# Dense products that read x alternately from its two halves, evictions that put the tokens back in order

## The chip, the core and the metric

The kernel runs on one core of a Trainium2 chip. The metric is the device time of the whole program in microseconds: the median of several runs. A profiled execution of the same program supplies the trace that is read here.

## What is computed

One inference step of a decoder layer, for 256 prompt tokens and 8 sample tokens together (264 tokens). Cut to what matters here, with every tensor in float32:

```
x += 0.5 * (silu(h @ w_gate) * (h @ w_up)) @ w_down      # h = rms_norm(x); w_gate, w_up 2048 x 5632
P  = rms_norm(x) @ w_in                                  # 2048 x 6400
mix = concat(attention(P), rwkv7(P), conv(P))
x += mix @ w_out                                         # 2048 x 2048
x += 0.5 * (silu(h @ w_gate2) * (h @ w_up2)) @ w_down2
```

The outputs are x for both groups of tokens and the new attention, RWKV and convolution states.

## The kernel before

The activations lie transposed in SBUF, features on partitions and the 264 tokens along the row: `xr` is x, `pj` the projection P, `hH` and `hL` the hidden layer, `mixH` and `mixL` the mixed heads. Each dense operand is held as two fp32r tensors, a high part and the rest (`xH` and `xL`, `wH` and `wL`), and a product is the sum of three matmuls: high with high, low with high, high with low (L378, L379, L380; or L339 for the part of the output projection that is prepared ahead during the RWKV stage).

Weights stream from HBM in chunks of up to 4 x 128 rows by 256 columns through a ring of four slots. For each chunk SyncE issues the load into `raw`, ScalarE makes `wH` (L310), VectorE makes `wL` (`tail`, L365), and TensorE works through it in `products`: for each of up to four row blocks q and two column halves, three matmuls, each with its own 128x128 weight load and the 264 tokens as moving operand. A chunk of 4 x 128 rows is 24 matmuls. The semaphore `tail_made` lets TensorE start a chunk; `chunk_used` frees the slot for ScalarE and the loads.

A gate/up pair is four chunks into PSUM banks 0 and 1 (gate) and four into banks 2 and 3 (up). An output pair of the down projection is twelve chunks, one of the input or output projection four. Banks alternate, so that a pair's results are read out while the next pair is being computed. The read-outs are on VectorE: `gate_scale` (L458, writes `gt`), `hidden` (L466, writes `ut`), `project` (L712, writes `pj`), `x_add` (L430, adds to `xr`) and `y_add` (L696, writes `yf` for the last stage). Each reads two banks of 264 columns. VectorE has one queue: tails and read-outs stand in it in the order of the program. Squares, heads and tails of x (`squares`, `x_heads`, `x_tails`) follow each `x_add`, and `turn_y` transposes each `yf` (L827, L829).

The dense matmuls already go through the tokens from the last column to the first: operand and output both have a step of -1. Other matmuls (the sums for the norm, attention, RWKV) go forwards; among them is L1183, a plain f32 product of a 128x128 block with 264 columns.

Of the kernel before, what the change touches and what calls it, by code (L numbers as in the profile page):

```python
# [20 lines left out]
ALU = mybir.AluOpType  # L21
# [8 lines left out]
N = T + NB  # L30
# [22 lines left out]
OUT_K0 = (0, 12, 4, 8)  # L53
# [57 lines left out]
def build(nc, t, o):  # L111
# [4 lines left out]
    def at(name, shape, dt, off):  # L116

        return nc.alloc_sbuf_tensor_at(name, shape, dt, offset=base + off)
# [5 lines left out]
    xr = at("xr", [P, KT, N], F32, 49152)  # L124
# [6 lines left out]
    gt = at("gt", [P, 2, N], F32, E0)  # L131
    st = at("st", [P, 2, N], F32, E0 + 2112)
    ut = at("ut", [P, 2, N], F32, E0 + 4224)
# [4 lines left out]
    rs = at("rs", [P, N], F32, K0)  # L138
# [16 lines left out]
    yf = at("yf", [P, 2, 2, N], F32, M0 + 92928 + 6144)  # L155
# [6 lines left out]
    pj = at("pj", [P, MT, N], F32, PB)  # L162
# [81 lines left out]
    def inner_slots(*ks):  # L244
# [18 lines left out]
    ahead = {k: (at(f"wH{k}", [P, CK, CW], F32R, hi), at(f"wL{k}", [P, CK, CW], F32R, lo))  # L263
             for k, hi, lo in ((0, F0, F0 + 8192), (1, F0 + 4096, PB + G), (2, L0 + 4 * HB, L0 + 4 * HB + 4096),
                               (3, L0 + 4 * HB + 8192, L0 + 4 * HB + 12288),
                               (6, PB + 2 * G, PB + 2 * G + 4096), (7, PB + 2 * G + 8192, PB + 2 * G + 12288))}
# [7 lines left out]
    ps = ctx.enter_context(nc.psum_tensor("ps", [P, 8, 512], F32))  # L274
    sems = {}

    def S(name):
        if name not in sems:
            sems[name] = ctx.enter_context(nc.semaphore(name))
        return sems[name]  # L280
# [13 lines left out]
    def number(first, per, i, k):  # L294

        return i * per + (first + k)
# [28 lines left out]
    def pe_ahead(pe, k, qs=range(CK)):  # L325

        pe.wait_ge(S("tail_made"), OUT + k + 1)
        for q in qs:
            for half in range(2):
                ahead_product(k, q, half, 0, mixH, k % 4 == 0 and q == 0)  # L330
                ahead_product(k, q, half, 0, mixL)
                last = ahead_product(k, q, half, 1, mixH, stop=k == 7 and q == CK - 1)
        if CK - 1 in qs:
            last.then_inc(S("chunk_used"), 1)

    def ahead_product(k, q, half, part, mix, start=False, stop=False):

        cols = slice(half * P, half * P + P)
        return nc.tensor.matmul(ps[:, 4 + k // 4 * 2 + half, 0:N][:, ::-1], ahead[k][part][:, q, cols],  # L339
                                mix[:, OUT_K0[k % 4] + q, :][:, ::-1], start=start, stop=stop)  # L340

    def pe_ahead_rwkv(pe):

# [18 lines left out]
    def tail(dve, nk, first, per, i, k):  # L362
# [3 lines left out]
                                wH[:, k % RING, 0:nk, :].bitcast(F32), ALU.subtract  # L366
                                ).then_inc(S("tail_made"), 1)

    def products(pe, vH, vL, k0, nk, bank, start, stop, first, per, i, k):

        pe.wait_ge(S("tail_made"), number(first, per, i, k) + 1)
        for q in range(nk):
            for half in range(2):
                cols = slice(half * P, half * P + P)
                out = ps[:, bank + half, 0:N][:, ::-1]
                high, low = vH[:, k0 + q, :][:, ::-1], vL[:, k0 + q, :][:, ::-1]
                a, b = start and q == 0, stop and q == nk - 1
                nc.tensor.matmul(out, wH[:, k % RING, q, cols], high, start=a, stop=False)  # L378
                nc.tensor.matmul(out, wH[:, k % RING, q, cols], low, start=False, stop=False)  # L379
                last = nc.tensor.matmul(out, wL[:, k % RING, q, cols], high, start=False, stop=b)  # L380
        last.then_inc(S("chunk_used"), 1)

    def two(ap):

        return ap[:].unsqueeze(1).broadcast_to([P, 2, N])
# [6 lines left out]
    def early(q):  # L392

        return isinstance(q, int) and q < 2
# [32 lines left out]
    def x_add(dve, w, q, bank, factor, used):  # L427

        dve.wait_ge(S("chunk_used"), used)
        nc.vector.scalar_tensor_tensor(xr[:, bass.ds(q * 2, 2), :], ps[:, bank:bank + 2, 0:N], factor,  # L430
                                       xr[:, bass.ds(q * 2, 2), :], ALU.mult, ALU.add
                                       ).then_inc(S("x_ready"), 1)

    def norm_sum(pe, w):

# [19 lines left out]

    def gate_scale(dve, u, first, p):
        dve.wait_ge(S("chunk_used"), first + 4 + p * GU_PER)
        nc.vector.tensor_tensor(gt[:], ps[:, 0:2, 0:N], two(rs), ALU.mult).then_inc(S("gate_scaled"), 1)  # L458

    def gate_silu(act, u, p):  # L460
        act.wait_ge(S("gate_scaled"), FT // 2 * u + 1 + p)
# [1 line left out]

    def hidden(dve, u, first, p):
        dve.wait_ge(S("chunk_used"), first + GU_PER + p * GU_PER)
        nc.vector.tensor_tensor(ut[:], ps[:, 2:4, 0:N], two(rs), ALU.mult).then_inc(S("up_scaled"), 1)  # L466
        dve.wait_ge(S("up_scaled"), FT // 2 * u + 1 + p)
        dve.wait_ge(S("silu_made"), FT // 2 * u + 1 + p)
        nc.vector.tensor_tensor(hf[:], st[:], ut[:], ALU.mult).then_inc(S("hidden_made"), 1)
# [171 lines left out]
    def dve_ffn(dve, u, gu, dn):  # L641
        def gate_up(i, first_pair):
            for k in range(RING if first_pair and u == 0 else 0, 4):
                tail(dve, CK, gu, GU_PER, i, k)
            if not first_pair:
                hidden(dve, u, gu, i - 1)
            elif u == 1:
                x_add(dve, 2, KT // 2 - 1, 6, 1.0, GU2)
            tail(dve, CK, gu, GU_PER, i, 4)
            if not first_pair:  # L650
                hidden_tail(dve, u, i - 1)
            elif u == 1:
                x_tails(dve, 2, KT // 2 - 1)
            for k in range(5, GU_PER):
                tail(dve, CK, gu, GU_PER, i, k)
            if first_pair:
                norm_reciprocal(dve, 2 * u)
            gate_scale(dve, u, gu, i)
# [32 lines left out]
    def y_add(dve, q, slot, used):  # L691

        dve.wait_ge(S("chunk_used"), used)
        if not early(q):
            dve.wait_ge(S("y_turned"), q - 1)
        nc.vector.scalar_tensor_tensor(yf[:, slot, :, :], ps[:, 4 + 2 * slot:6 + 2 * slot, 0:N], 0.5,  # L696
                                       xr[:, bass.ds(q * 2, 2), :], ALU.mult, ALU.add
                                       ).then_inc(S("x_ready"), 1)

    def column_pair(q):  # L700

# [2 lines left out]
    def seat(q):  # L704

        return 2 * column_pair(q) + (-6 if 16 <= q < 19 else 6 if q >= 22 else 0)

    def project(dve, q, bank):

        dve.wait_ge(S("chunk_used"), IN + IN_PER + q * IN_PER)  # L710
        c = seat(q)
        nc.vector.tensor_tensor(pj[:, c:c + 2, :], ps[:, bank:bank + 2, 0:N], two(rs), ALU.mult  # L712
                                ).then_inc(S("projected"), 1)

    def dve_in(dve):
        for k in range(4):
            tail(dve, CK, IN, IN_PER, 0, k)
        x_add(dve, 1, KT // 2 - 1, 6, 0.5, IN)
        x_tails(dve, 1, KT // 2 - 1)
        for k in range(4):  # L720
# [55 lines left out]
    def pe_ffn(pe, u, gu, dn):  # L776
        w = 2 * u

        def gate_up(i, first_pair):
            for k in range(GU_PER):  # L780
                if first_pair and k < 4:
                    pe.wait_ge(S("x_tail"), 16 * w + 4 * (k + 1))
                if k == 0 and not first_pair:
                    pe.wait_ge(S("gate_scaled"), FT // 2 * u + i)
                if k == 4 and not first_pair:
                    pe.wait_ge(S("up_scaled"), FT // 2 * u + i)
                products(pe, xH, xL, CK * (k % 4), CK, 0 if k < 4 else 2, k % 4 == 0, k % 4 == 3,
                         gu, GU_PER, i, k)
                if first_pair and u == 0 and k == 0:
                    pe_turn_x(pe, 6)  # L790
                    pe_turn_x(pe, 7)
                if first_pair and k == (5 if u == 0 else 3):
                    norm_sum(pe, w)

        def down(i, jj, first_pair):
            q = i * 2 + jj
            if not (isinstance(i, int) and i == 0):
                pe.wait_ge(S("x_ready"), 8 * (w + 1) - 1 + q)
            for k in range(DN_PER):
                if first_pair:  # L800
                    pe.wait_ge(S("hidden_tail"), FT // 2 * u + (DN_K0[k] + DN_KT[k] + 1) // 2)
                products(pe, hH, hL, DN_K0[k], DN_KT[k], 4 + 2 * jj, k == 0, k == DN_PER - 1,
                         dn + DN_PER * jj, 2 * DN_PER, i, k)
                if u == 1 and not first_pair and k == 5:
                    turn_y(pe, q - 1, 1 - jj)
# [26 lines left out]
    def pe_in(pe):  # L832
        for k in range(4):
            pe.wait_ge(S("x_tail"), 16 + 4 * (k + 1))
            products(pe, xH, xL, CK * k, CK, 0, k == 0, k == 3, IN, IN_PER, 0, k)
# [1651 lines left out]
```

## Time and profile before

| | |
|---|---|
| median of 3 runs | 2109.93 us (2109.79 to 2113.65) |
| span of the profiled execution | 2106.7 us |
| TensorE busy | 2074.8 us, 98% |
| VectorE busy | 1183.1 us, 56% |
| ScalarE busy | 880.0 us, 42% |
| mean load rate from HBM and to it | 177 GB/s |

The page gives no other time of the profiled execution than its span; the median stands 3.2 us above it. Matmuls are pipelined: one of 284 ns starts every 120 ns or so, so that a busy share of TensorE says little, and the distance from one start to the next says more. The span falls into gate and up of the first FFN (to about 541 us), its down projection (to 802), the input projection with attention beside it (to about 1065), the RWKV stage (to 1256), the output projection (to 1339), and the second FFN (gate and up to 1838, down to 2101).

### The profile page before, as it was taken

How to read it: one execution, taken by the hardware profiler on the slowest of the kernel's cores; microseconds unless marked ns; L12 is line 12 of the kernel's file. 1: busy time of each engine (PE TensorE's matmuls, PEld its weight loads, DVE VectorE, ACT ScalarE, POOL GpSimd, SP SyncE). 2: the span in 40 equal slices, each digit the busy share in tenths (PEclk: the TensorE clock that was granted, in tenths of full speed). 3: DMA queues.
4: the chain of work that ended last, by engine and by line, in shares of the span. 5: the costliest groups of instructions: out<-in, count | busy, mean ns of one | idle time of the engine just before them, and what ended most of it. 6: DMA issues, size and time to landing. Idle time of an engine off the chain costs nothing.

```text
span 2106.7 us, 44887 instructions
## 1 busy us (share of the span) xinstructions
PE 2074.8 (98%) x18520; PEld 2038.6 (97%) x18520; DVE 1183.1 (56%) x1203; ACT 880.0 (42%) x1004; POOL 196.9 (9%) x160
## 2 busy tenths in 40 slices
PE   8999999999999999999998999999999999999999
PEld 7999999999999999999986899999999999999999
DVE  6555555555444545568996575555555555544443
ACT  5444444444434434434345444444444444433333
POOL 4000000000000000015401871000000000000000
PEclk9999999999999999999998999999999999999999
DMA  5655555665555556668873055555556555556553
GB/s 184 197 182 180 179 180 179 185 182 180 176 179 177 187 172 199 175 201 221 238 237 88 4 165 190 180 180 180 181 179 186 179 179 180 183 166 196 185 176 125
DMA packets 361375, 373.43 MB, mean 177 GB/s; under 512 B 13321, under 2 KB 353837, under 8 KB 361190
## 3 DMA queue, kind: packets, MB, share of 16 engines
q1 hardware_dynamic: 352288, 350.53, 53.5%
q0 software_dynamic: 5424, 15.39, 3.1%
q10 hardware_dynamic: 3582, 6.33, 0.9%
q8 instruction: 63, 1.03, 0.2%
q14 instruction: 18, 0.15, 0.0%
HBM read 366.89 MB, written 5.32 MB: 177 GB/s over the span
## 4 chain that ended last, share of the span: by engine, by line
PE 89%; DVE 5%; DMA 3%; ACT 1%; POOL 1%; issue 1%; ACTq 0%; SPq 0%; POOLq 0%; DVEq 0%
PE ps L378 28%; PE ps L380 28%; PE ps L379 28%; DMA raw<-in_w_in_dram 2%; DVE wL L365 2%; DVE wL L323 1%; POOL acc L888 1%; PE ps L1266 1%; PE ps L1955 0%; DMA vb<-in_cache_swa_v_dram 0%; ACT wH L310 0%; PE ps L1958 0%; DMA xin<-in_x_prompt_dram 0%; PE ps L1966 0%; PE ps L339 0%
## 5 line engine op out<-in xcount | busy, mean ns | idle before, releaser
L365 DVE TENSOR_TENSOR wL<-raw,wH 128x1024 fp32r<-128x1024 f32 (+1 forms) x668 | 824.2, 1240 | 829.3 <-ACT wH L310 828.5
L310 ACT ACTIVATE wH<-raw 128x1024 fp32r<-128x1024 f32 (+1 forms) x668 | 691.2, 1037 | 966.4 <-PE ps L380 888.0
L378 PE MATMUL ps<-xH,wH 128*128 128x264 f32 x3616 | 1030.2, 285 | 6.2 <-DVE wL L365 5.8
L380 PE MATMUL ps<-xH,wL 128*128 128x264 f32 x3616 | 1027.3, 284 | 0.0
L379 PE MATMUL ps<-xL,wH 128*128 128x264 f32 x3616 | 1027.2, 284 | 0.0
L378 PEld LDWEIGHTS ps<-xH,wH 128*128 128x128 f32 x3616 | 681.3, 188 | 11.3 <-issue 9.7
L380 PEld LDWEIGHTS ps<-xH,wL 128*128 128x128 f32 x3616 | 681.1, 188 | 0.0
L379 PEld LDWEIGHTS ps<-xL,wH 128*128 128x128 f32 x3616 | 680.5, 188 | 0.2
L378 PE MATMUL ps<-hH,wH 128*128 128x264 f32 x1408 | 402.4, 286 | 0.0
L380 PE MATMUL ps<-hH,wL 128*128 128x264 f32 x1408 | 401.4, 285 | 0.0
L379 PE MATMUL ps<-hL,wH 128*128 128x264 f32 x1408 | 401.3, 285 | 0.0
L378 PEld LDWEIGHTS ps<-hH,wH 128*128 128x128 f32 x1408 | 265.0, 188 | 0.2
L379 PEld LDWEIGHTS ps<-hL,wH 128*128 128x128 f32 x1408 | 265.1, 188 | 0.0
L380 PEld LDWEIGHTS ps<-hH,wL 128*128 128x128 f32 x1408 | 264.6, 188 | 0.0
L462 ACT ACTIVATE st<-gt 128x528 f32<-128x528 f32 x44 | 28.5, 647 | 83.6 <-DVE gt L458 83.6
L888 POOL TENSOR_TENSOR acc<-acc,sq 128x528 f32<-128x528 f32 x21 | 34.9, 1663 | 278.0 <-ACT sq L406 277.0
L378 PE MATMUL ps<-mixH,wH 128*128 128x264 f32 x192 | 54.5, 284 | 0.0
L379 PE MATMUL ps<-mixL,wH 128*128 128x264 f32 x192 | 54.5, 284 | 0.0
L380 PE MATMUL ps<-mixH,wL 128*128 128x264 f32 x192 | 54.5, 284 | 0.0
L890 POOL COPY acc<-sq 128x528 f32<-128x528 f32 x3 | 2.7, 894 | 552.5 <-ACT sq L406 549.7
L421 DVE SCALAR_TENSOR_TENSOR xL<-xr,vcol,xH 128x264 fp32r<-128x264 f32 (+1 forms) x48 | 29.9, 664 | 15.6 <-ACT xH L413 15.4
L380 PEld LDWEIGHTS ps<-mixH,wL 128*128 128x128 f32 x192 | 36.1, 188 | 0.0
(377 smaller groups left out, 1140.3 us busy)
## 6 DMA issues: line engine op xcount, KB each, us to landing
raw<-in_ffn_w_gate_dram SPq DMA_DIRECT2D x176, 512.0 KB, 3.5
raw<-in_ffn_w_up_dram SPq DMA_DIRECT2D x176, 512.0 KB, 3.5
raw<-in_ffn_w_down_dram SPq DMA_DIRECT2D x128, 512.0 KB, 3.3
raw<-in_w_in_dram SPq DMA_DIRECT2D x100, 512.0 KB, 4.9
raw<-in_ffn_w_down_dram SPq DMA_DIRECT2D x64, 384.0 KB, 2.8
raw<-in_w_out_dram SPq DMA_DIRECT2D x32, 512.0 KB, 4.4
kb<-in_cache_swa_k_dram POOLq DMA_DIRECT2D x24, 256.0 KB, 6.6
vb<-in_cache_swa_v_dram ACTq DMA_DIRECT2D x24, 256.0 KB, 6.4
```

Of the source, the lines that this page charges most:

```text
L310: nc.scalar.activation(wH[:, k % RING, 0:nk, :], raw[:, k % RING, 0:nk, :], ACT.Copy).then_inc(S("head_made"), 1)
L323: nc.vector.tensor_tensor(low[:], raw[:, k % RING], high[:].bitcast(F32), ALU.subtract).then_inc(S("tail_made"), 1)
L365: nc.vector.tensor_tensor(wL[:, k % RING, 0:nk, :], raw[:, k % RING, 0:nk, :], wH[:, k % RING, 0:nk, :].bitcast(F32), ALU.subtract).then_i ...
L378: nc.tensor.matmul(out, wH[:, k % RING, q, cols], high, start=a, stop=False)
L379: nc.tensor.matmul(out, wH[:, k % RING, q, cols], low, start=False, stop=False)
L380: last = nc.tensor.matmul(out, wL[:, k % RING, q, cols], high, start=False, stop=b)
L421: nc.vector.scalar_tensor_tensor(xL[:, bass.ds(q * 2 + e, 1), :], xr[:, bass.ds(q * 2 + e, 1), :], vcol[:, 0, bass.ds(q * 2 + (16 * w + e) ...
L462: nc.scalar.activation(st[:], gt[:], ACT.Silu).then_inc(S("silu_made"), 1)
L888: nc.gpsimd.tensor_tensor(acc[:], acc[:], sq[:, slot, :, :], ALU.add).then_inc(S("squares_added"), 1)
L890: nc.gpsimd.tensor_copy(acc[:], sq[:, 0, :, :]).then_inc(S("squares_added"), 1)
L1266: last = nc.tensor.matmul(ps[rows, 4, :], pS[:, g, b, :], vb[:, b % 3, g, :], start=g == 0, stop=g == 2)
```

## The change

In `products` and `ahead_product`, the moving operand is read from the last column to the first with the two halves of the tokens taking turns: 263, 131, 262, 130, down to 132, 0. `two_ways` makes that access pattern. PSUM is written as before, column 263 first and column 0 last, each neighbour to neighbour. So bank columns 2c and 2c+1 hold tokens c and 132+c. The five read-outs read every second column (`by_token`) and write two runs of 132 tokens (`by_way`), which puts the tokens in their order. `x_add` and `y_add` become two VectorE instructions each, one for each bank. Nothing else is changed: loads, splits, semaphores and the order of the queues are the same.

```
     def ahead_product(k, q, half, part, mix, start=False, stop=False):
-        return nc.tensor.matmul(ps[:, 4 + k // 4 * 2 + half, 0:N][:, ::-1], ahead[k][part][:, q, cols],
-                                mix[:, OUT_K0[k % 4] + q, :][:, ::-1], start=start, stop=stop)
+        return nc.tensor.matmul(ps[:, 4 + k // 4 * 2 + half, 0:N][:, ::-1].rearrange("p (c way) -> p c way", way=2), ahead[k][part][:, q, cols],
+                                two_ways(mix[:, OUT_K0[k % 4] + q, :]), start=start, stop=stop)
...
+    def two_ways(ap):
+        return ap[:, ::-1].rearrange("p (way c) -> p c way", way=2)
+
+    def by_token(bank):
+        return ps[:, bank:bank + 2, 0:N].rearrange("p e (c way) -> p e way c", way=2)
+
+    def by_way(ap):
+        return ap.rearrange("p e (way c) -> p e way c", way=2)
...
-                out = ps[:, bank + half, 0:N][:, ::-1]
-                high, low = vH[:, k0 + q, :][:, ::-1], vL[:, k0 + q, :][:, ::-1]
+                out = ps[:, bank + half, 0:N][:, ::-1].rearrange("p (c way) -> p c way", way=2)
+                high, low = two_ways(vH[:, k0 + q, :]), two_ways(vL[:, k0 + q, :])
...
     def x_add(dve, w, q, bank, factor, used):
-        nc.vector.scalar_tensor_tensor(xr[:, bass.ds(q * 2, 2), :], ps[:, bank:bank + 2, 0:N], factor,
-                                       xr[:, bass.ds(q * 2, 2), :], ALU.mult, ALU.add
-                                       ).then_inc(S("x_ready"), 1)
+        for e in range(2):
+            tile = by_way(xr[:, bass.ds(q * 2 + e, 1), :])[:, 0]
+            last = nc.vector.scalar_tensor_tensor(tile, by_token(bank)[:, e], factor, tile, ALU.mult, ALU.add)
+        last.then_inc(S("x_ready"), 1)
...
-        nc.vector.tensor_tensor(gt[:], ps[:, 0:2, 0:N], two(rs), ALU.mult).then_inc(S("gate_scaled"), 1)
+        nc.vector.tensor_tensor(by_way(gt[:]), by_token(0), by_way(two(rs)), ALU.mult).then_inc(S("gate_scaled"), 1)
...
-        nc.vector.tensor_tensor(ut[:], ps[:, 2:4, 0:N], two(rs), ALU.mult).then_inc(S("up_scaled"), 1)
+        nc.vector.tensor_tensor(by_way(ut[:]), by_token(2), by_way(two(rs)), ALU.mult).then_inc(S("up_scaled"), 1)
...
-        nc.vector.scalar_tensor_tensor(yf[:, slot, :, :], ps[:, 4 + 2 * slot:6 + 2 * slot, 0:N], 0.5,
-                                       xr[:, bass.ds(q * 2, 2), :], ALU.mult, ALU.add
-                                       ).then_inc(S("x_ready"), 1)
+        for e in range(2):
+            last = nc.vector.scalar_tensor_tensor(by_way(yf[:, slot])[:, e], by_token(4 + 2 * slot)[:, e], 0.5,
+                                                  by_way(xr[:, bass.ds(q * 2 + e, 1), :])[:, 0], ALU.mult, ALU.add)
+        last.then_inc(S("x_ready"), 1)
...
-        nc.vector.tensor_tensor(pj[:, c:c + 2, :], ps[:, bank:bank + 2, 0:N], two(rs), ALU.mult
+        nc.vector.tensor_tensor(by_way(pj[:, c:c + 2, :]), by_token(bank), by_way(two(rs)), ALU.mult
                                 ).then_inc(S("projected"), 1)
```

## Rows read from the trace of the kernel before

**Rows 1.** The page: span, and busy time of each engine
```profile
span 2106.7 us, 44887 instructions
...
PE 2074.8 (98%) x18520; PEld 2038.6 (97%) x18520; DVE 1183.1 (56%) x1203; ACT 880.0 (42%) x1004; POOL 196.9 (9%) x160
```

**Rows 2.** Busy time by stretches: length, then each engine, granted clock, DMA share, GB/s
```profile
48.00:540.00 492.00, 492.00 (x4071) 492.00 (x4072) 264.77 (x258) 204.09 (x214) 0.00 (x0) 1.00 0.60 183
545.00:800.00 255.00, 255.00 (x2092) 255.00 (x2091) 124.03 (x119) 104.75 (x120) 13.63 (x9) 1.00 0.56 180
930.00:1065.00 135.00, 128.88 (x1069) 125.80 (x1068) 116.23 (x105) 52.67 (x65) 56.58 (x57) 1.00 0.84 240
```

**Rows 3.** Waits: who waited for whom, us in total, times, longest
```profile
ACT wH L310 <- PE ps L380: 888.0, 542, 3.7
DVE wL L365 <- ACT wH L310: 828.5, 575, 6.1
...
PE ps L378 <- DVE wL L365: 5.8, 5, 2.5
```

**Rows 4.** Groups of instructions by form, whole span
```profile
L378 PE MATMUL ps<-xH,wH 128*128 128x264 f32 x3616 | 1030.2, 285 | 6.2 <-DVE wL L365 5.8
L378 PE MATMUL ps<-hH,wH 128*128 128x264 f32 x1408 | 402.4, 286 | 0.0
L378 PE MATMUL ps<-mixH,wH 128*128 128x264 f32 x192 | 54.5, 284 | 0.0
L712 DVE TENSOR_TENSOR pj<-ps,rs 128x528 f32<-128x528 f32 x25 | 17.5, 700 | 11.4 <-PE ps L380 11.3
L430 DVE SCALAR_TENSOR_TENSOR xr<-ps,xr 128x528 f32 x12 | 8.4, 700 | 0.0
L339 PE MATMUL ps<-mixH,wH 128*128 128x264 f32 x64 | 16.2, 292 | 2.1 <-DVE wL L323 2.0
```

**Rows 5.** Busy time by stretches, as rows 2, in short windows
```profile
15.30:19.00 3.70, 3.70 (x17) 3.70 (x18) 3.17 (x6) 2.63 (x5) 0.00 (x0) 0.50 0.53 164
100.00:200.00 100.00, 100.00 (x830) 100.00 (x829) 52.42 (x51) 41.34 (x43) 0.00 (x0) 1.00 0.59 179
600.00:700.00 100.00, 100.00 (x821) 100.00 (x821) 49.18 (x48) 41.08 (x47) 5.38 (x3) 1.00 0.56 182
1700.00:1800.00 100.00, 100.00 (x830) 100.00 (x829) 54.32 (x54) 41.77 (x44) 0.00 (x0) 1.00 0.59 180
```

**Rows 6.** Chain that ended last, 886 to 889 us: start, duration, what
```profile
887.02 1.78 PE ps L1183 x8
```

**Rows 7.** Timeline from 304.4 us, TensorE and VectorE
```profile
304.60 1.22 DVE L365 TENSOR_TENSOR wL<-raw,wH 128x1024 fp32r<-128x1024 f32 x1 [1.72 <-ACT wH L310]
...
305.18 0.29 PE L379 MATMUL ps<-xL,wH 128*128 128x264 f32 x1
305.31 0.29 PE L380 MATMUL ps<-xH,wL 128*128 128x264 f32 x1
305.44 0.28 PE L378 MATMUL ps<-xH,wH 128*128 128x264 f32 x1
```

**Rows 8.** Single lines of VectorE: duration min/median/max in ns, starts, form
```profile
L2377 DVE COPY yo<-ps x1: 245/245/245, 1220.7 to 1220.7; 128x48 f32<-128x48 f32 x1
L1360 DVE COPY vcol<-ps x1: 221/221/221, 878.2 to 878.2; 128x68 f32<-128x68 f32 x1
L1381 DVE COPY qkr<-ps x1: 277/277/277, 930.1 to 930.1; 96x128 f32<-96x128 f32 x1
L1808 DVE SCALAR_TENSOR_TENSOR kk<-ps,vcol,pj x6: 482/482/485, 1133.7 to 1135.7; 128x264 f32<-128x264 f32 x6
```

**Rows 9.** Timeline from 2101 us
```profile
2101.39 0.71 DVE L696 SCALAR_TENSOR_TENSOR yf<-ps,xr 128x528 f32<-128x528 f32 x1 [6.95 <-PE ps L380]
```

**Rows 10.** Groups of TensorE, 930 to 1065 us
```profile
L378 PE MATMUL ps<-xH,wH 128*128 128x264 f32 x323 | 92.6, 287 | 3.6 <-DVE wL L365 3.5
```

## Prediction

> **What bounds the kernel now.** I read the page first: span and engine shares [rows 1]. TensorE is busy 98% of 2106.7 us; VectorE 56%, ScalarE 42%. Busy time of pipelined matmuls doesn't tell whether the engine is at its limit, so I went to the table by stages [rows 2]. In gate/up (the second FFN repeats the first) TensorE is busy every microsecond, 4071 matmuls in 492 us, 120.9 ns from one to the next; in the down stretches 2092 in 255 us, 121.9 ns, all at the full granted clock (1.00). The waits of TensorE say the same from the other side: over the whole run L378 waits 5.8 us for VectorE's low halves [rows 3]. While it streams, nothing holds it up but its own pace. The exception is 930 to 1065 us (end of the input projection beside attention): the DMA share is 0.84, TensorE is idle for 6 us [rows 2], and 3.5 of the 5.8 us of waiting fall there [rows 10].
>
> The reader is to see one number: the **pitch** of a dense matmul, start to start. There are 3 x (3616 + 1408 + 192 + 64) = 15,840 of them (each count is that of one of three equal rows, shown for L378 and L339) [rows 4]. One hundred undisturbed microseconds hold 830 (120.5 ns) in gate/up and 821 (121.8 ns) in down [rows 5]. So the dense products take about 1,915 of 2,107 us, and 1 ns of pitch is worth 15.8 us. Everything else in this change is small beside that.
>
> **What the pitch is made of.** 264 columns at 2.4 GHz, one a period, are 110 ns. Three rows stand around the measured 120.5.
> - At the half clock (granted 0.50, so 1.2 GHz) 17 of the same instructions fall into 3.7 us [rows 5], some 218 ns each. 264/1.2 is 220: no excess at all.
> - The plain f32 product of the same shape (L1183: 128x128 stationary, 264 columns, own weight load, read forwards) takes 1.78 us for eight [rows 6], 222.5 ns, or twice 111. It needs two periods for a column and has 1 ns of excess per 264 periods.
> - The dense product at full clock wants a new 4-byte column each period and pays 120.5: 9.3 ns above 111.2.
>
> So the excess shows only where operands are wanted at the highest rate. It also moves with SBUF traffic of others: against the 120.5 of the average, starts stand 0.13 us apart (305.18, 305.31, 305.44) half a microsecond after VectorE's tail (raw and wH in, wL out) has started at 304.60 [rows 7]. The excess therefore looks like fetching, not counting. The order of the moving read is what the change alters.
>
> **The change, part by part.**
>
> 1. Moving read. For each of the 15,840 matmuls, column 263 comes first, then 131, then 262, 130 and so on: neighbours in the stream stand 528 bytes apart instead of 4. Number of columns, bytes, weight loads, start/stop flags and waits are unchanged. The trace has no dense matmul with such a read, so I bound its price. From below: the whole excess goes, -9.3 ns each, pitch 111.2. From above: each column takes two periods, as the columns of L1183 do and as those at the half clock do: 220 ns [rows 5, 6]. VectorE gives a hint for the upper end: its copy of 48 values to places 1056 bytes apart takes 245 ns (L2377), while contiguous copies out of PSUM take 221 ns for 68 values (L1360) and 277 for 128 (L1381) [rows 8]. A contiguous value costs 1.06 ns there: (700 - 277)/(528 - 128), from L430 [rows 4] and L1381. At that slope 48 contiguous values would take 200 ns, so L2377 pays 45 ns more: 0.9 ns per far-stepped value, nearly one more of its own steps. This is a write of another engine; no row has a far-stepped read on TensorE.
>
> The Trainium skill (Advanced Engine Details and Errata, section Memory Cachelines) speaks against this change: SBUF is read in lines of 16 bytes, and at least two hits on a line are needed to absorb its latency, with a penalty when each access is to another line. By it every column here would be a new line, and the pitch would be the upper end. The row of VectorE agrees with its direction, no row here tests it for TensorE.
>
> For the other side: now one walk through x advances by a value in every period. The alternate order makes two walks, one per half, and each advances only every second period. If the engine can keep a place in both, whatever it fetches per walk has twice the time, and the 9.3 ns shrink. I take half of them, 4.6 ns, as the likeliest gain, because no row lies between no effect and all: pitch 115.9 in gate/up.
>
> 2. PSUM write. Still column 263 down to 0, neighbours adjacent, same bank: the access pattern is merely written as pairs. 0.
>
> 3. Evictions in token order. gt, ut (44 each) and pj (25) keep their count; they read PSUM at a step of two values. Now 700 ns each (pj, and the others in the same form) [rows 4]; between +0 and, at a further period for each value as above, +0.55 us. In gate/up that is at most 2 x 0.55 in the 23.2 us of a pair (192 x 120.9 ns), of which VectorE is busy 54% (264.8 of 492) [rows 2]; it would be 59%. What stands behind them in VectorE's queue is the next chunk's tail, and tails wait 828.5 us in total for ScalarE, who waits 888.0 for TensorE [rows 3]: each has over a microsecond of slack in 2.9. Cost 0; if that cover were gone, at most 113 x 0.55 = 62 us.
>
> 4. x_add (16) and y_add (8) become two instructions of 264 values. Now 700 ns; the nearest 264-value instruction on PSUM, L1808, is 482 ns, six of them start 2.0 us from first to last, 0.4 apart [rows 8]. Two are about 0.88 us, +0.2 each, 5 us of VectorE in all. 23 lie beside products (the bank they free is wanted a whole column pair later). The last y_add doesn't: TensorE ends, yf takes 0.71, the turn waits for it [rows 9]. +0.2, and up to +0.5 for the PSUM step. I take +0.5 in sum with the two stage changes.
>
> 5. DMA, semaphores, POOL: untouched. If TensorE speeds up by 4%, the 180 GB/s of gate/up become 187; 240 have been moved in 930 to 1065 [rows 2]. In that stretch, though, its 970 dense products (3 x 323) [rows 10] share the queues with 240 GB/s of loads, and TensorE already waits for tails; I count no gain.
>
> **Sum.** 14,870 x -4.6 ns = -68.4; +0.5; span 2106.7 becomes 2038.8. The median 2109.9 of the runs lies 3.2 above the profiled span (the page has no other time of that execution), so 2042.
>
> **Rivals.**
> - A, faster (the forecast). For it: the 9.3 ns exist, vanish at the half clock, and grow when VectorE uses SBUF. Against: no row shows that a second place can be held. Own range 1980 (all but 1 ns of excess gone: 14,870 x -8.5 = -126) to 2100. Chance 0.45.
> - B, half-rate read, on the other side. Each column is a fetch of its own and TensorE gets one every second period: pitch 220 for all that now have 121.2 on average. 15,840 x 98.8 = +1565, 3675; if a third of the present 9.3 ns stays on top of it, 49 us more, 3725. It decides as soon as what the engine holds of x serves only neighbours in the stream. For it: the write of L2377. Against: it is another engine's. Everything else would be hidden beneath it: the load rate falls to about 100 GB/s. Chance 0.35. It is also what the line rule of the Trainium skill named above would do here.
> - C, the order doesn't matter, the excess belongs to something else (for one, to swapping weights): +0.5 us, 2110.4. For it: three stretches far apart, with 16 different rows of x, weights from four slots and loads landing all the time, hold 830, 821 and 830 products [rows 5]; collisions of addresses would scatter more. Chance 0.12.
> - D, more collisions without half rate: every product takes what those beside VectorE's tails take now, 125 instead of 121: +4 x 15,840 = +63, 2173. Chance 0.08.
>
> **How the numbers follow.** 0.2% of the time is 4.2 us, about what a measurement of this kernel can tell from no change. A and its whole range give faster; B and D slower; C same: 0.45, 0.12, 0.43. Leaving out B would leave out more than 2 in 10, so the range reaches from A's low end to B: 1980 to 3730. It is wide because the outcomes are two islands; A's own range is 1980 to 2100.
>
> **What would show it.** The decisive view is the count of matmuls in 100 us of gate/up: 830 now; 863 for A, about 455 for B, 830 for C, 800 for D, with the clock still granted in full. In down: 821 becomes 853 or about 455. The duration of a single matmul (284 ns) would shrink by the same 4.6 ns in A and grow by 100 in B. VectorE's gt, ut and pj at 700 show part 3 right; at 1.25 us, its upper bound. x_add in two pieces near 0.45 shows part 4. In B the waits of ScalarE for TensorE would more than double from 888 us and the idle 6 us of 930 to 1065 vanish. The prediction is wrong at its root if the pitch goes up: then half of the excess wasn't there to take, and the read pays for every far step.

## Result and the profile after

The changed kernel takes 1987.95 us (median of 4 runs, 1986.01 to 1989.46) against 2109.96 before: a ratio of 0.9417, 95% interval 0.9404 to 0.943, or 122 us less. That is the direction of rival A and lies in its own range of 1980 to 2100, near the lower end: the gain is 1.8 times the 68 us that were forecast. The profiled execution has a span of 1984.2 us.

The page of the changed kernel, busy time by engine:

```profile
span 1984.2 us, 44915 instructions
PE 1942.3 (98%) x18520; PEld 1904.6 (96%) x18520; DVE 1183.9 (60%) x1227; ACT 881.5 (44%) x1004; POOL 196.7 (10%) x160
```

The number of matmuls is the same (18,520), VectorE has 24 instructions more and the same busy time (1183.1 before [rows 1]). TensorE is 98% busy in both kernels, so the busy share doesn't show the gain at all. The count of matmuls in a stretch does. Busy time by stretches of the changed kernel (length, then TensorE, weight loads, VectorE, ScalarE, POOL, granted clock, DMA share, GB/s):

```profile
48.00:540.00 492.00, 492.00 (x4375) 492.00 (x4375) 282.46 (x276) 219.97 (x231) 1.15 (x1) 1.00 0.64 196
545.00:730.00 185.00, 185.00 (x1647) 185.00 (x1646) 97.47 (x99) 81.51 (x93) 10.64 (x6) 1.00 0.60 194
```

and in windows of 100 us, which answer to [rows 5]:

```profile
100.00:200.00 100.00, 100.00 (x892) 100.00 (x891) 56.17 (x54) 44.40 (x47) 0.00 (x0) 1.00 0.63 194
600.00:700.00 100.00, 100.00 (x891) 100.00 (x890) 52.14 (x53) 43.11 (x49) 5.36 (x3) 1.00 0.59 193
1600.00:1700.00 100.00, 100.00 (x892) 100.00 (x891) 57.60 (x57) 45.26 (x47) 0.00 (x0) 1.00 0.65 194
```

In 492 us there are 4375 matmuls instead of 4071 [rows 2], so the pitch fell from 120.9 to 112.5 ns (a window counts those that reach over its edges too, so over 100 us the quotient comes out 0.3 to 0.4 ns too small: the starts themselves were 120.8 and 122.0 ns apart on average where the quotients of [rows 5] give 120.5 and 121.8). Gate/up and down now have the same pitch; before, down was 1 ns slower. And it no longer varies. Timeline of the changed kernel, TensorE beside a tail of VectorE:

```profile
305.17 0.28 PE L391 MATMUL ps<-xL,wH 128*128 128x264 f32 x1
305.28 0.28 PE L392 MATMUL ps<-xH,wL 128*128 128x264 f32 x1
305.40 0.28 PE L390 MATMUL ps<-xH,wH 128*128 128x264 f32 x1
305.51 0.28 PE L391 MATMUL ps<-xL,wH 128*128 128x264 f32 x1
305.62 0.28 PE L392 MATMUL ps<-xH,wL 128*128 128x264 f32 x1
305.67 1.22 DVE L365 TENSOR_TENSOR wL<-raw,wH 128x1024 fp32r<-128x1024 f32 x1 [1.48 <-ACT wH L310]
305.73 0.28 PE L390 MATMUL ps<-xH,wH 128*128 128x264 f32 x1
305.85 0.28 PE L391 MATMUL ps<-xL,wH 128*128 128x264 f32 x1
305.96 0.28 PE L392 MATMUL ps<-xH,wL 128*128 128x264 f32 x1
```

Starts are 0.11 or 0.12 us apart before and during the tail; the 0.13 of [rows 7] are gone. In the starts of the trace from 100 to 200 us and from 600 to 700 us, every gap is 112 or 113 ns; before, they were 118 to 129. 264 columns at 2.4 GHz are 110 ns, so 2.5 ns are left above one column a period. (The Trainium skill, TensorE: Matmul & The Clock Gate, section Back-to-back issue gap, gives N/2.4 + 2.5 ns as the gap of an isolated matmul at the full clock, and says that a stream in which each matmul has its weight load departs from it. By the isolated rule 264 columns give 112.5 ns; this stream, with a weight load for each matmul, shows just that.)

**The variation before was not VectorE's doing.** The prediction took the 0.13 us beside a tail for traffic of VectorE. Starts stand as far apart in the down projection with VectorE idle. Timeline of the kernel before, TensorE and VectorE:

```profile
755.50 1.22 DVE L365 TENSOR_TENSOR wL<-raw,wH 128x1024 fp32r<-128x1024 f32 x1 [1.45 <-ACT wH L310]
...
756.77 0.29 PE L378 MATMUL ps<-hH,wH 128*128 128x264 f32 x1
756.90 0.28 PE L379 MATMUL ps<-hL,wH 128*128 128x264 f32 x1
...
757.51 0.28 PE L378 MATMUL ps<-hH,wH 128*128 128x264 f32 x1
...
757.69 1.23 DVE L365 TENSOR_TENSOR wL<-raw,wH 128x1024 fp32r<-128x1024 f32 x1 [0.96 <-ACT wH L310]
```

From 756.77 to 757.51 there are six matmuls, 123 ns each, and VectorE does nothing from 756.72 to 757.69. In gate/up the gaps repeat every 96 matmuls, which is four chunks, once through the 16 rows of x and the four slots of the ring: their standard deviation is 1.7 ns over all and 0.1 ns among those at the same place of this cycle (matmuls 400 to 4,200 of the trace). In down they repeat every 264, once through the 44 rows of the hidden layer: 2.3 ns over all, 0.3 at the same place. In gate/up two thirds of all gaps are exactly 120 ns. At two places half a cycle apart the gap is 122.7 and 122.6 ns on average, though VectorE works at the first in all of 41 rounds and at the second in none. Beside tails the mean is 121.4 ns and with VectorE idle 120.3, because the tails come at the same places of the cycle each time, and those are among the slow ones. So in gate/up the excess over two walks is 7.5 ns (120 less 112.5) at most places, and up to 7 ns more at some, which goes with the operands of that place. In down only one gap in eight is 120 ns, and more are above it. Whether the row of x, the place of the weights or something else that repeats with them makes the difference wasn't looked into.

**Where the 122 us come from.** The first sum for the norm of each stage (L439 before, L452 after) marks the stages. It starts at 804.63 and 1339.15 us before:

```profile
804.63 0.61 PE L439 MATMUL ps<-acc,ones 128*128 128x264 f32 x2
...
1339.15 0.61 PE L439 MATMUL ps<-acc,ones 128*128 128x264 f32 x2
```

and at 749.88 and 1271.14 after:

```profile
749.88 0.39 PE L452 MATMUL ps<-acc,ones 128*128 128x264 f32 x1
...
1271.14 0.61 PE L452 MATMUL ps<-acc,ones 128*128 128x264 f32 x2
```

Up to the first mark 54.8 us are saved; between the marks (input projection, RWKV stage, output projection) 534.5 have become 521.3, 13.3 less; behind the second, up to the end of the span, 767.5 have become 713.1, 54.5 less. Together 122.5.

The middle gives less than its share. Groups of TensorE in the stretch up to 1065 us before and up to 1003 us after, which hold the same 1,952 dense products:

```profile
L378 PE MATMUL ps<-xH,wH 128*128 128x264 f32 x651 | 186.5, 287 | 3.6 <-DVE wL L365 3.5
```

```profile
L390 PE MATMUL ps<-xH,wH 128*128 128x264 f32 x651 | 183.3, 282 | 10.7 <-DVE wL L365 10.5
```

The first took 260 us (from 805), the second 252.5 (from 750.5): 7.5 us less, where 1,952 x 8.4 ns would be 16.4. Busy time by stretches shows what took the rest. Before and after:

```profile
805.00:1065.00 260.00, 253.88 (x2089) 250.18 (x2088) 191.16 (x166) 103.84 (x112) 59.35 (x62) 1.00 0.73 211
```

```profile
750.50:1003.00 252.50, 241.49 (x2086) 237.02 (x2086) 190.53 (x165) 102.63 (x111) 59.07 (x62) 0.99 0.75 217
...
867.00:1003.00 136.00, 124.99 (x1068) 121.10 (x1067) 115.98 (x104) 51.96 (x64) 56.31 (x57) 0.97 0.83 238
...
930.70:936.60 5.90, 5.86 (x27) 5.89 (x28) 5.90 (x3) 1.82 (x2) 5.10 (x4) 0.50 0.92 259
```

All of the loss is in the second part. By their starts, the 984 products up to 930 us before (867 after) gave 8.3 us, 8.4 ns each. The 968 products behind them, the stretch of 930 to 1065 us before [rows 2], took 136.1 us instead of 135.1: nothing gained, and 1 us lost. TensorE is idle for 11.0 instead of 6.1 us there: a faster consumer waits more for the tails (10.5 instead of 3.5 us), while its wait for attention's scores fell from 2.6 to 0.3 us. Waits in that part of the changed kernel:

```profile
ACT wH L310 <- DMA raw<-in_w_in_dram: 70.2, 26, 8.4
...
DVE wL L365 <- ACT wH L310: 19.5, 9, 7.1
...
PE ps L390 <- DVE wL L365: 10.5, 9, 2.9
```

ScalarE waits for the loads, VectorE for ScalarE, and TensorE for VectorE. The stretch moved 240 GB/s before and moves 238 now, so it looks bound by its loads and not by the pitch; no run tests that. VectorE also has attention's instructions ahead of some tails in its queue: one of 1.75 us stands right before the tail that starts at 929.38. Behind one of these waits the granted clock is 0.50 (1.2 GHz), and matmuls start 0.22 us apart; TensorE had stood idle for 2.9 us just before:

```profile
927.61 0.28 PE L392 MATMUL ps<-xH,wL 128*128 128x264 f32 x1
930.74 0.56 PE L390 MATMUL ps<-xH,wH 128*128 128x264 f32 x1 [2.85 <-DVE wL L365]
931.09 0.42 PE L391 MATMUL ps<-xL,wH 128*128 128x264 f32 x1
...
933.95 0.42 PE L392 MATMUL ps<-xH,wL 128*128 128x264 f32 x1
934.17 0.42 PE L390 MATMUL ps<-xH,wH 128*128 128x264 f32 x1
```

27 of them at 220 instead of 112.5 ns are 2.9 us. 4.9 and 2.9 account for 7.8 of the 8.9 us that are missing (16.4 less 7.5); the last microsecond isn't explained.

### The profile page after: what moved, and what is told of

Its sections match the earlier page's. It is cut to its first block, busy times and chain, and to the rows that moved or that the text cites. A ratio compares the mean times of both kernels' runs of the same rounds, so it can differ in the third digit from the quotient of the medians.

```text
span 1984.2 us, 44915 instructions
## 1 busy us (share of the span) xinstructions
PE 1942.3 (98%) x18520; PEld 1904.6 (96%) x18520; DVE 1183.9 (60%) x1227; ACT 881.5 (44%) x1004; POOL 196.7 (10%) x160
## 4 chain that ended last, share of the span: by engine, by line
PE 88%; DVE 6%; DMA 3%; ACT 1%; issue 1%; POOL 1%; ACTq 0%; SPq 0%; DVEq 0%; POOLq 0%
PE ps L390 27%; PE ps L392 27%; PE ps L391 27%; DVE wL L365 3%; DMA raw<-in_w_in_dram 2%; DVE wL L323 1%; POOL acc L902 1%; PE ps L1280 1%; PE ps L1969 0%; DMA vb<-in_cache_swa_v_dram 0%; PE ps L1972 0%; DMA xin<-in_x_prompt_dram 0%; ACTq L1340 0%; PE ps L1980 0%; ACT wH L310 0%
## 5 line engine op out<-in xcount | busy, mean ns | idle before, releaser
L390 PE MATMUL ps<-xH,wH 128*128 128x264 f32 x3616 | 1004.2, 278 | 14.7 <-DVE wL L365 14.5
L391 PE MATMUL ps<-xL,wH 128*128 128x264 f32 x3616 | 1000.0, 277 | 0.0
L392 PE MATMUL ps<-xH,wL 128*128 128x264 f32 x3616 | 999.9, 277 | 0.0
L390 PE MATMUL ps<-hH,wH 128*128 128x264 f32 x1408 | 389.2, 276 | 0.0
L391 PE MATMUL ps<-hL,wH 128*128 128x264 f32 x1408 | 388.6, 276 | 0.0
L392 PE MATMUL ps<-hH,wL 128*128 128x264 f32 x1408 | 388.6, 276 | 0.0
L390 PEld LDWEIGHTS ps<-mixH,wH 128*128 128x128 f32 x192 | 36.3, 189 | 0.0
```

## Experiments

Each edit changes only the access patterns of the dense matmuls, in `products` and `ahead_product`. `read` makes the moving operand from a row of x (264 values) and `write` the place in PSUM; before, both are `ap[:, ::-1]`. Where the two don't match and the read-outs don't put it right, the tokens come out in the order of the stream and are scaled by the norms of others; what is timed is the same work: as many matmuls of the same shape. e9 to e12 read some tokens twice and others not at all. All but e4 were run once, so their differences are read from the pitch: the verdict is the count of matmuls in gate/up, 100 to 200 us. The question behind them: what about the alternate order is it that counts?

### e1: one walk, forwards

```
-    return ap[:, ::-1]        # read and write
+    return ap
```

> Dense products read x and write PSUM from the first column to the last, one walk, everything else as before. Theory S (the stream's order): what the engine holds of x while it fetches is used up by neighbours in the stream; the direction of a single walk is of no account, pitch 120 to 122 ns, time within 20 us of before. Rival N (the negative step is itself a part of the gain): pitch above 122 ns, 123 to 130, 2140 to 2220 us.

2123.8 us (before beside it 2111.7).

```profile
100.00:200.00 100.00, 100.00 (x819) 100.00 (x818) 53.24 (x52) 40.96 (x44) 0.00 (x0) 1.00 0.58 178
600.00:700.00 100.00, 100.00 (x826) 100.00 (x825) 49.52 (x47) 41.08 (x48) 5.42 (x3) 1.00 0.56 183
```

819 in 100 us: the starts are 122.5 ns apart on average in gate/up (120.8 before), and 121.4 in down, where it is a little faster than before (122.0; 826 against 821). The direction of one walk is worth 12 us, a tenth of what the second walk is worth. That lies within theory S's 20 us and below theory N's 2140, but the direction isn't quite of no account; why backwards is better in one stage and worse in the other wasn't looked into.

### e2: the order of before, in two levels

```
+    return ap[:, ::-1].rearrange("p (c two) -> p c two", two=2)     # read and write
```

> The order of before (263, 262, 261, ...) written as a two-level access pattern of 132 pairs, for x and for PSUM, with the read-outs of before. It tells the form of the instruction from the order of the tokens. If the order is the cause: 830 matmuls in 100 us of gate and up, 120.5 ns, 2110 us. If the two-level pattern itself were the cause: 112.5 ns, 1988 us.

2110.9 us.

```profile
100.00:200.00 100.00, 100.00 (x830) 100.00 (x829) 53.59 (x52) 40.74 (x43) 0.00 (x0) 1.00 0.58 182
```

830, exactly as before. The form of the access pattern does nothing; the order does.

### e3: two walks, forwards

From the changed kernel, `two_ways` and `out` (`ahead_product` alike):

```
-    return ap[:, ::-1].rearrange("p (way c) -> p c way", way=2)
+    return ap.rearrange("p (way c) -> p c way", way=2)
...
-    out = ps[:, bank + half, 0:N][:, ::-1].rearrange("p (c way) -> p c way", way=2)
+    out = ps[:, bank + half, 0:N].rearrange("p (c way) -> p c way", way=2)
```

> The two halves still take turns, but both walks and PSUM run from the first column to the last (0, 132, 1, 133, ...), with the read-outs of the changed kernel. Theory S: 112.5 ns, 1988 us, as backwards. Rival N: the backward walk is needed for a part of it, 114 to 120 ns, 2010 to 2100 us.

1987.5 us.

```profile
100.00:200.00 100.00, 100.00 (x892) 100.00 (x891) 56.20 (x54) 44.41 (x47) 0.00 (x0) 1.00 0.64 194
```

With two walks the direction is of no account: 892 as in the changed kernel.

### e4: the read-outs alone

The changed kernel's read-outs with the products of before.

```
...
+    out = ps[:, bank + half, 0:N][:, ::-1]
+    high, low = vH[:, k0 + q, :][:, ::-1], vL[:, k0 + q, :][:, ::-1]
```

> x is read as before; only the read-outs are those of the changed kernel (every second column of PSUM, x_add and y_add in two pieces), so they leave the tokens permuted. It gives the price of the read-outs by themselves. The prediction has +0.5 us, ratio 1.000; if the step of two values cost VectorE a further period a value, gt would take 1.25 us and the time rise by 1 to 10 us.

2109.7 us; the ratio to before is 0.9994, 95% interval 0.9984 to 1.0004. Groups of VectorE in it:

```profile
L479 DVE TENSOR_TENSOR ut<-ps,rs 128x528 f32<-128x528 f32 x44 | 30.9, 701 | 0.0
L471 DVE TENSOR_TENSOR gt<-ps,rs 128x528 f32<-128x528 f32 x44 | 30.8, 701 | 0.1
...
L444 DVE SCALAR_TENSOR_TENSOR xr<-ps,xr 128x264 f32 (+1 forms) x32 | 12.2, 423 | 0.0
L710 DVE SCALAR_TENSOR_TENSOR yf<-ps,xr 128x264 f32<-128x264 f32 x16 | 6.1, 424 | 6.9 <-PE ps L392 6.9
```

Reading every second column of PSUM costs VectorE nothing that shows: 701 ns against 700 [rows 4]. The halves of x_add and y_add take 423 each. So the whole gain is the products'. That it is the read's, and not the pattern in PSUM's, e9 and e10 show below: they change the read alone and have all of it.

### e5 to e8: what must not be far, and from what

Four other orders of the read, everything else as before. The rival theories, in the names of the expectations: L, two lanes that take the values of the stream in turn, each holding the piece of 16 bytes that it used last; H, one holder of the last two pieces; B, collisions of neighbours in the same place.

```
e5  read: ap[:, ::-1].rearrange("p (way c two) -> p c way two", way=2, two=2)
e6  read: ap[:, ::-1].rearrange("p (c way) -> p way c", way=2)
e7  read: ap[:, ::-1].rearrange("p (c way) -> p way c", way=4)
e8  read: ap[:, ::-1].rearrange("p (way c) -> p c way", way=4)
```

> The two halves take turns by pairs of tokens (263, 262, 131, 130, 261, 260, ...); PSUM and the read-outs as before, so the tokens come out in the order of the stream, scaled by other tokens' norms. Theory L (two lanes: values 0, 2, 4, ... of the stream are fetched by one lane and 1, 3, 5, ... by another, and each holds the one 16-byte piece of x that it used last): each lane now jumps between the halves with every value, 264 fetches instead of 132 of before and 66 of after: well above 120.5 ns, up to 220, 2200 to 3700 us. Theory H (the engine holds the last two pieces, whichever value asks): 66 fetches as after, 112.5 ns, 1988 us. Theory B (neighbours of the stream that lie in the same place collide): between before and after, 116 ns, 2050 us.

2903.6 us, 581 in 100 us, 173 ns:

```profile
100.00:200.00 100.00, 100.00 (x581) 100.00 (x580) 37.22 (x37) 29.21 (x31) 0.00 (x0) 1.00 0.41 127
```

> One walk over every second token, then one over the others (263, 261, ..., 1, 262, ..., 0; 8 bytes between neighbours, two values of each 16-byte piece in a row); PSUM and read-outs as before, tokens left in the stream's order. Theory L: each lane takes one value of a piece, 264 fetches, as slow as e5. Theory H: 132 fetches, about the 120.5 ns of before. Theory B: other places, 112.5 to 116 ns.

3993.5 us, 417 in 100 us:

```profile
100.00:200.00 100.00, 100.00 (x417) 86.75 (x416) 26.24 (x26) 21.38 (x22) 0.00 (x0) 1.00 0.29 89
```

and its timeline, 0.24 us from start to start at the full clock (more than half of the gaps are exactly 240 ns, the mean is 241):

```profile
299.82 0.44 PE L387 MATMUL ps<-xL,wH 128*128 128x264 f32 x1
300.06 0.44 PE L388 MATMUL ps<-xH,wL 128*128 128x264 f32 x1
300.30 0.44 PE L386 MATMUL ps<-xH,wH 128*128 128x264 f32 x1
```

> One walk over every fourth token, four times (16 bytes between neighbours, each value in another 16-byte piece); PSUM and read-outs as before, tokens left in the stream's order. Theories L and H both: 264 fetches, well above 120.5 ns, up to 220 ns and 3700 us, and for L the same as e6. Theory B: 112.5 ns, since no two neighbours share a piece.

4038.6 us, 411 in 100 us, 244 ns:

```profile
100.00:200.00 100.00, 100.00 (x411) 85.94 (x410) 25.95 (x25) 20.32 (x21) 0.00 (x0) 1.00 0.29 90
```

> Four quarters of the tokens take turns (263, 197, 131, 65, 262, ...; 264 bytes between neighbours); PSUM and read-outs as before, tokens left in the stream's order. Theory L: each lane alternates between two quarters, 264 fetches, as slow as e5. Theory H: four walks are more than two held pieces, 264 fetches. Theory B: 112.5 ns as after, or less if room is left below it.

2442.2 us, 701 in 100 us, 143 ns:

```profile
100.00:200.00 100.00, 100.00 (x701) 100.00 (x700) 45.48 (x45) 34.41 (x36) 0.00 (x0) 1.00 0.50 153
```

e6 decides against H: two neighbours of its stream share a 16-byte piece, as those of before do, yet it takes twice as long. e7 and e6 decide against B: none of e7's neighbours share a place, and it is the slowest. In both each value of the stream is 16 bytes or more from the one two places before it, and both take 240 to 244 ns: nearly as slow as each other, as L has it, and slower still than the 220 that was given as its end. But L also wants e5 and e8 to be as slow, and they are not. So L holds in part: in a single walk the distance between value s and value s + 2 of the stream counts. Where value s + 2 lies in another walk the price is in between. Either something beyond the last piece is kept, or fetches overlap in part; the runs don't tell these apart.

### e9 to e12: does the distance between the walks count?

```
e9   read: offset + 259, steps [-1, 132], [-128, 2]
e10  read: offset + 135, steps [-1, 132], [-4, 2]
e11  read: offset + 77,  steps [-1, 66],  [-4, 4]
e12  read: offset + 139, steps [-2, 66],  [-8, 2], [-1, 2]
```

> Two walks of 132 as after, but 128 tokens (512 bytes) apart instead of 132 (528 bytes): 259, 131, 258, 130, ...; tokens 128 to 131 are read twice and 260 to 263 not at all; PSUM and read-outs as before. Theory L (each of two lanes takes every second value of the stream and does best on a walk of 4-byte steps): the distance is of no account, 112.5 ns, 1988 us. Rival P (the two places must lie in different parts of SBUF, which 528 bytes bring about and a round distance may not): above 112.5, up to the 240 of the single walk.

1987.1 us:

```profile
100.00:200.00 100.00, 100.00 (x891) 100.00 (x890) 56.18 (x54) 44.42 (x46) 0.00 (x0) 1.00 0.65 194
```

> Two walks as after, only 4 tokens (16 bytes) apart: 135, 131, 134, 130, ...; tokens 4 to 131 are read twice, those from 136 on not at all; PSUM and read-outs as before. Theory L: 112.5 ns, 1988 us, as 528 bytes. Rival P: the two walks are always in neighbouring pieces, as the single walks of e6 and e7 were, which took 240 ns: above 120.5.

1987.8 us:

```profile
100.00:200.00 100.00, 100.00 (x891) 100.00 (x890) 56.30 (x55) 44.37 (x46) 0.00 (x0) 1.00 0.63 194
```

> Four walks as in e8 (143 ns), but 4 tokens (16 bytes) apart instead of 66: 77, 73, 69, 65, 76, ...; tokens 0 to 77 are read again and again, the rest not; PSUM and read-outs as before. Each lane changes between two pieces 32 bytes apart. e8 was quicker than the 240 ns of e6 and e7, though each lane needs a new piece for each value there too. Theory F (fetches overlap where they go to places far apart): here they are near, about 240 ns, 4000 us. Theory M (a lane remembers a little more than its last piece, wherever it lies): 143 ns as e8, 2440 us.

2428.0 us:

```profile
100.00:200.00 100.00, 100.00 (x705) 100.00 (x704) 45.14 (x44) 34.51 (x37) 0.00 (x0) 1.00 0.49 152
```

> Pairs take turns as in e5 (172 ns), but the two walks are 8 tokens (32 bytes) apart instead of 132: 139, 138, 131, 130, 137, ...; tokens 0 to 139 are read, most of them twice, the rest not; PSUM and read-outs as before. Theory F: about 240 ns, 4000 us. Theory M: 172 ns as e5, 2900 us.

2898.6 us:

```profile
100.00:200.00 100.00, 100.00 (x582) 100.00 (x581) 37.23 (x37) 29.46 (x31) 0.00 (x0) 1.00 0.42 128
```

At the distances tried it hardly counts: 528, 512 and 16 bytes give 892, 891 and 891; four walks give 701 and 705, which is 1 ns; pairs 581 and 582. Theory P falls, and so does theory F, by which only far places would overlap. What counts is how the stream is dealt out, not where in SBUF the walks are.

### What the twelve say together

| order | from value s to value s + 2 | pitch |
|---|---|---|
| two walks (the change, e3, e9, e10) | 4 bytes | 112.5 ns |
| one walk (before, e2; e1) | 8 bytes | 120.8; 122.5 ns |
| every second token (e6) | 16 bytes | 241 ns |
| every fourth token (e7) | 32 bytes | 244 ns |
| four walks (e8, e11) | other walk; s + 4 is 4 bytes on | 143, 142 ns |
| pairs in turn (e5, e12) | other walk; s + 4 is 8 bytes on | 173, 172 ns |

Suppose that even and odd values of the stream are fetched separately, in pieces of 16 bytes. Then a row of 264 values costs 66 fetches in two walks, 132 in one, 264 in e6. The commonest gap of e6, 240 ns, over 264 is 0.91 ns a fetch; 132 of them are 120.0 ns, the commonest gap of before in gate/up, and 66 are 60 ns, less than the 110 that the columns take, so that the columns set the pace. One number, taken from e6, fits the first three rows of the table. It is a model and not a thing the trace shows: no row shows a fetch, and no run varies the number of columns, the type or the weight loads. It has e7 at 240 too, where 244 were measured, it says nothing of the direction (e1), and the last two rows would need 157 and 189 fetches by it; what makes these cheaper than 264 stays open.

The Trainium skill (Advanced Engine Details and Errata, section Memory Cachelines) has two hits on a 16-byte line as what absorbs the latency. Its size fits e6 (no second hit, twice the time). But by the model hits must be counted among every second value of the stream. Neighbours needn't share a line (e10, the change: 112.5 ns), and with two hits (before) 8.4 ns are still lost, which four take away.

## Why the prediction was right, and where its size was off

- **The direction was a bet that came in.** The prediction gave faster a chance of 0.45 and the half-rate read 0.35, with a range from 1980 to 3730 us that holds both, and said itself that no row showed its condition, that the engine can keep a place in both walks.
- **What bounds the kernel.** Right: the pitch. 122 us came of a pitch that is 8.4 ns less in gate/up and 9.5 in down. At 15.8 us for each ns it would have been more; waits took some of it back (see the sum).
- **The excess is fetching.** Right for the order of the read, by e1 to e4 and e9. Of the prediction's three signs the two without excess at half rate stand [rows 5, 6]. The third, that it grows beside VectorE's tails [rows 7], was misread: the 0.13 us belong to a place in a cycle of 96 matmuls and come with VectorE idle as well. Rival D took its 125 ns from that sign.
- **Part 1, moving read: the term that was mis-sized.** The prediction took 4.6 ns, half of the 9.3, "because no row lies between no effect and all". Measured are 8.4 to 9.5 ns. There was no ground for the half: if, as in the model above, the pitch is the longer of two paces, the fetches' and the columns', then fetches that fall below the columns' pace take all their excess with them at once. A maximum of two paces gives no halves. Its lower bound of 111.2 ns was right to 1.3 ns.
- **"It makes two walks, each with twice the time": half right.** Two walks taken in turn value by value do give all of it. But an engine that merely keeps a place in each walk would do as well with pairs in turn (e5), and, if it can keep four, with four walks (e8), and these take 173 and 143 ns. What the runs show in its place: the order counts by the step from each value of the stream to the next but one, and is best where that is 4 bytes. That the change happened to deal out the halves in just this way was luck as far as the prediction's reasoning goes.
- **Rival B, half rate.** Wrong for this order, right as a mechanism: e6 and e7 are its 220 ns and some more (240, 244). The point that it named, whether what is held serves only neighbours of the stream, was the right question, and the answer is that it serves every second one. The line rule of the Trainium skill (Advanced Engine Details and Errata, section Memory Cachelines), as the prediction read it, would have given that time to this change, and the measurement decides against that reading. C and D fell with the count of 892.
- **Part 2, PSUM: 0**, borne out by e2. An alternate order in PSUM as well, which would spare the read-outs their work, wasn't tried.
- **Parts 3 and 4, the read-outs.** The prediction had +0.5 us; e4 has 0.9994 (0.9984 to 1.0004), which can't tell 0.5 us from none. The bounds from VectorE's far-stepped write were much too high for a step of two values in PSUM. The two halves of y_add take 0.77 together instead of 0.71 at the end, not 0.88.
- **Part 5, no gain in 930 to 1065 us.** Right: the same 968 products took 136.1 us instead of 135.1. What their pitch was worth went into longer waits for the tails and one fall of the clock.
- **The sum.** Forecast: 14,870 x -4.6 + 0.5 = -68. At the measured pitches the 11,616 products outside the down projections are worth 8.4 ns each and the 4,224 inside them 9.5: 137.7 us. The spans show 122.5. Of the 15.2 that are missing, 8.9 were given back in the stretch around 930 to 1065 us, as shown above. By the same reckoning 4.4 went between its end and the second mark: 1,216 products (352 of the input projection, 768 of the output projection and the first 96 of the second FFN) are worth 10.2 us, against 13.3 - 7.5 = 5.8. By the starts of the same products in both traces, nearly all of that went between 1065 and 1256 us, in the RWKV stage. The remaining 1.9 went before the first mark and behind the second.

## What to carry over

Where TensorE streams fp32r matmuls and their pitch is well above columns over clock, look at the order in which the moving operand is read. Here two interleaved contiguous walks cost less than one, and a single walk in steps of 8 or 16 bytes cost twice as much. More walks, or pairs in turn, were worse than one. A step of two values in the PSUM reads of VectorE was free, so the order can be put right there. Before an excess is halved in a forecast, ask whether it is a sum or a maximum: once the larger of two paces has fallen below the other, the whole excess is gone. Before a gap in a timeline is put down to what runs beside it, look for the same gap where nothing runs beside it. And what a faster engine gains, it loses again where it is fed just in time: here 968 products gained nothing at all.

## What was unexpected of the hardware

- One contiguous walk isn't the fastest read of fp32r for TensorE: 120.8 ns backwards and 122.5 forwards in gate/up, against 112.5 for two walks, at each of the three distances tried, 16, 512 and 528 bytes.
- 8 bytes between neighbours of the stream (e6, 241 ns) are far worse than 528 (the change, 112.5).
- With one walk backwards the gaps between starts, 118 to 129 ns, follow the operands and not VectorE's traffic (a fixed cycle of 96 matmuls in gate/up, of 264 in down); with two walks they are 112 or 113 ns in gate/up and down.
